# Where two head norms stand in VectorE's order: in front of a weight split or behind the running sums

## The reference, cut to what matters

```python
def _stick_breaking(q, k, v):
    for blk in range(seq // SB_BLOCK):
        ...
        z = jnp.einsum("bthd,bshd->bhts", qb, kb).astype(jnp.float32) * scale
        log_1m = jnp.where(causal, jax.nn.log_sigmoid(-z), 0.0)
        log_survive = lax.cumsum(log_1m, axis=3, reverse=True) - log_1m
        w = jnp.where(causal, jnp.exp(jax.nn.log_sigmoid(z) + log_survive), 0.0)
        outs.append(jnp.einsum("bhts,bshd->bthd", w.astype(vb.dtype), vb))

def _sb_mix(h, mem_n, w_in, q_g, k_g, w_out, mem_w_kv, mq_g, mk_g):
    q, k, v, q_mem = jnp.split(h @ w_in, [SB_WIDTH, 2 * SB_WIDTH, 3 * SB_WIDTH], axis=-1)
    q = _rmsnorm(q.reshape(shp), q_g)      # 12 heads of 128
    k = _rmsnorm(k.reshape(shp), k_g)
    o = _stick_breaking(q, k, v.reshape(shp)).reshape(b, s, SB_WIDTH)
    o_mem = _memory_attention(q_mem, mem_n, mem_w_kv, mq_g, mk_g)
    return jnp.concatenate([o, o_mem], axis=-1) @ w_out
```

## Time and profile before

| | |
|---|---|
| median of three runs | 805.43 us (805.22 to 806.25) |
| profiled execution, whole | 805.58 us |
| its span | 803.8 us |
| TensorE (PE) busy | 793.8 us, 99% of the span |
| VectorE (DVE) busy | 609.1 us, 76% |
| ScalarE (ACT) busy | 437.4 us, 54% |
| GpSimd (POOL) busy | 62.9 us, 8% |
| granted TensorE clock | 0.999 of full speed over the span |

### The profile page before, as it was taken

One profiled execution on the slowest core, in us unless ns is written; L12 is line 12 of the kernel. 1 busy time (PEld: TensorE's weight loads), 2 busy tenths in 40 slices (PEclk: granted clock), 3 DMA queues, 4 the chain that ended last, 5 costly groups with the idle time before them and its releaser, 6 DMA issues.

```text
span 803.8 us, 9752 instructions
## 1 busy us (share of the span) xinstructions
PE 793.8 (99%) x3778; PEld 663.4 (83%) x3778; DVE 609.1 (76%) x906; ACT 437.4 (54%) x520; POOL 62.9 (8%) x80
## 2 busy tenths in 40 slices
PE   9989999999999999999999999999999999999998
PEld 7977888888888888888888888888888888888886
DVE  6678989998757688889447968588666778888742
ACT  6657776366636445444426576757743644445430
POOL 4000003540000000000000000113220000000000
PEclk9999999999999999999999999999999999999999
DMA  7845366544445666665565644443435565665551
GB/s 245 287 145 173 107 215 217 176 135 147 157 158 179 190 207 190 187 200 198 176 202 166 201 157 157 157 131 132 150 130 169 180 206 178 192 209 188 180 208 52
DMA packets 85293, 141.38 MB, mean 176 GB/s; under 512 B 3406, under 2 KB 50672, under 8 KB 85248
## 3 DMA queue, kind: packets, MB, share of 16 engines
q1 hardware_dynamic: 84256, 139.60, 53.3%
q10 hardware_dynamic: 608, 1.06, 0.4%
q0 software_dynamic: 384, 0.11, 0.1%
HBM read 139.68 MB, written 1.07 MB: 175 GB/s over the span
## 4 chain that ended last, share of the span: by engine, by line
PE 79%; DVE 12%; ACT 3%; issue 3%; DMA 2%; SPq 0%; DVEq 0%; ACTq 0%
PE acc L1294 24%; PE acc L1296 24%; PE acc L1295 24%; DVE lo L952 4%; PE bank L1291 3%; DVE zs L1065 2%; DMA raw<-in_ssd_w_in 2%; ACT hi L632 1%; DVE seg L1085 1%; DVE seg L1093 1%; PE bank L1488 1%; PE bank L1466 1%; DVE hg L1085 1%; ACT sq L632 1%; ACT zs L632 1%
## 5 line engine op out<-in xcount | busy, mean ns | idle before, releaser
L952 DVE TENSOR_TENSOR lo<-raw,hi 128x2048 fp32r<-128x2048 f32 (+2 forms) x132 | 296.5, 2252 | 91.3 <-ACT hi L632 90.0
L632 ACT ACTIVATE hi<-raw 128x2048 fp32r<-128x2048 f32 (+2 forms) x132 | 244.7, 1861 | 95.9 <-DMA raw<-in_ffn_w_gate_up 44.3
L1294 PE MATMUL acc<-lo,aT_hi 128*128 128x512 f32 (+1 forms) x672 | 262.5, 391 | 1.5 <-DVE lo L952 1.2
L1296 PE MATMUL acc<-hi,aT_lo 128*128 128x512 f32 (+1 forms) x672 | 258.9, 385 | 0.0
L1295 PE MATMUL acc<-hi,aT_hi 128*128 128x512 f32 (+1 forms) x672 | 258.5, 385 | 0.0
L1294 PEld LDWEIGHTS acc<-lo,aT_hi 128*128 128x128 f32 x672 | 126.3, 188 | 26.9 <-issue 1.4
L1296 PEld LDWEIGHTS acc<-hi,aT_lo 128*128 128x128 f32 x672 | 126.2, 188 | 25.3
L1295 PEld LDWEIGHTS acc<-hi,aT_hi 128*128 128x128 f32 x672 | 126.4, 188 | 24.2
L1172 DVE STREAM_TRANSPOSE uT<-un 32x256 f32<-32x256 f32 x160 | 69.7, 436 | 2.6
L1294 PE MATMUL acc<-lo,uT_hi 128*128 128x512 f32 x176 | 68.8, 391 | 0.0
L1295 PE MATMUL acc<-hi,uT_hi 128*128 128x512 f32 x176 | 68.6, 390 | 0.0
(11 more groups left out here) (203 smaller groups left out, 845.3 us busy)
## 6 DMA issues: line engine op xcount, KB each, us to landing
raw<-in_ffn_w_gate_up SPq DMA_DIRECT2D x88, 512.0 KB, 4.8
raw<-in_ffn_w_down SPq DMA_DIRECT2D x22, 1024.0 KB, 4.9
raw<-in_sb_w_in SPq DMA_DIRECT2D x20, 1024.0 KB, 5.1
raw<-in_ssd_w_in SPq DMA_DIRECT2D x14, 1024.0 KB, 5.3
raw<-in_mem_w_kv SPq DMA_DIRECT2D x8, 1024.0 KB, 5.0
raw<-in_ssd_w_out SPq DMA_DIRECT2D x8, 1024.0 KB, 4.9
raw<-in_sb_w_out SPq DMA_DIRECT2D x8, 1024.0 KB, 4.9
seg<-cs_rows SPq DMA_DIRECT2D x6, 384.0 KB, 4.9
```

The source lines that it names most:

```text
L632: return nc.scalar.activation(out_, in_, func, **k)
L952: v.tensor_tensor(lo[w % RING][:, c], raw[w % RING][:, c], hi[w % RING][:, c].bitcast(F), ALU.subtract).then_inc(lo_ready, 1)
L1294: mm(ps, stat_hi, mov_lo, start=first, stop=False)
L1296: return mm(ps, stat_lo, mov_hi, start=False, stop=last)
```

## The change

The norms of q1 and q2 get a kind of their own, "hl", which is not in `EARLY` and so comes in list order, last in its unit. The other eight norms stay "hn". The function that is called is the same.

```diff
+LATE_NORMS = ["q1", "q2"]
 HEAD_NORMS = ["qm0", "km0", "km1", "qm1", "k0", "k1", "k2", "q0", "q1", "q2"]
...
     for n in HEAD_NORMS:
-        at(block_end("dtq1" if n == "qm0" else n) + 1, ("hn", n))
+        at(block_end("dtq1" if n == "qm0" else n) + 1, ("hl" if n in LATE_NORMS else "hn", n))
...
-NO_BANK = ("gate", "silu", "seg", "segm", "pn", "dt", "memsq", "memnorm", "sps", "zd", "hn", "tq", "ts")
+NO_BANK = ("gate", "silu", "seg", "segm", "pn", "dt", "memsq", "memnorm", "sps", "zd", "hn", "hl", "tq", "ts")
...
-                elif kind == "hn":
+                elif kind in ("hn", "hl"):
                     head_norm(step[1])
```

## The result

The changed kernel takes 812.62 us (median of 6 runs, 812.50 to 815.24), the kernel before 805.60 us in the same comparison (805.22 to 806.57). The ratio is 1.0093, 95% interval 1.0082 to 1.0103: **7 us slower**, where no measurable difference was forecast (805.5, range 804.4 to 806.7). The profiled execution has 812.50 us and a span of 810.7 us.

The account below looks back on a forecast made before the run. TensorE was taken to bound the kernel, with one removable wait at `O`: -0.81 us won, +0.86 for both groups of transposes held by longer norms, +0.05 in sum, giving 805.5 us, range 804.4 to 806.7.

Parts of the forecast that it names:

- What bounds the kernel: TensorE, busy 99%; its one wait at 500 to 625 us, 0.6 us before `O`, traced through masks to q1's norm.
- Gain of up to 0.81 us: Unit 83's subtractions and masks come earlier, `O` starts unhindered at 530.92, q1's transposes at 532.22 instead of 533.03.
- Norms later: Norms of q1 and q2 start behind the subtractions; their transposes, ready at 531.63 and 564.00, have 0.59 us to spare.
- what is late next: Behind the norms: L1200, L1201, split, `spb` masks, `sp_hi`, `sp_lo`; until 571.7 in unit 88, hidden by 0.5 us.
- What eats the 0.59 us: GpSimd's masks fall into both late norms; two small VectorE instructions pass in 1.42 us, making the norm 1.02 us longer.
- d: What the masks add to a late norm: 1.02 us forecast, 0 to 1.42 as bounds; transposes max(0, d - 0.59) late.
- Rival 3: Both masks run back to back, VectorE gets nothing through, 1.42 us added per norm: +0.85, 806.3 us; chance 0.16.
- rival 4: Small norm instructions keep GpSimd's masks out until the norm ends; `O` 1.35 and 2.1 us later, 808.9 us; chance 0.04.

Follow-up runs that it names:

- the last run: Against the kernel before: in unit 83 the two subtractions of C, and `zd` of unit 84, go ahead of the split of unit 85; 804.77 us against 805.55, ratio 0.9991.

## Why the prediction was wrong, point by point

**What bounds the kernel: right but for one link.** One wait of TensorE, worth 0.8 us at most, caused by the norm ahead of the subtractions: the trace of the last run is shorter by 0.78. But `O` in unit 84 had a second condition beside the masks, and the trace of before has a sign of it, in a view that the prediction does not use. The waits of the weight loads (PEld) of the kernel before, 500 to 625 us, have one row, and the timeline has that load:

```profile
PEld bank L1488 <- DVE spb L1201: 1.0, 1, 1.0
```

```profile
531.62 0.30 PEld L1488 LDWEIGHTS bank<-lsb,vn 128*128 128x128 f32 x2 [0.97 <-DVE spb L1201]
```

The row names VectorE's `spb`. That is no operand of `O`, and by the code only the bank ties the two. It is not what the load waited for in the end: the first L1201 was done at 530.78, the masks at 531.55, 0.07 before the load. So the prediction's reading of that one wait, the masks, holds; what it missed is the tie, which was met 0.14 us before `O` was due at 530.92 and so had next to no room for a later `zd`.

**Gain of up to 0.81 us: right in size, not reached here.** The masks end in time, but the wait that took the place of the old one is longer.

**"Norms later": the failing step.** It asked who waits for the norm, found the transposes with 0.59 us to spare, and left the queue behind the norm to "what is late next". There L1200 and L1201 are named, but followed only through what they write, `spb`, the masks, `sp_hi` and `sp_lo` to the next sums. They also free what they read. For unit 88 the prediction even has `zd` end at 567.0, and compares that only with the sums at 572.18. A late `zd` was put at nothing for `O`; it made `O` 2.7 us late in each place. With the bank as a condition the prediction's own numbers give the result: norm to 532.50, then 1.1 for the first two instructions of `zd`, 533.6 against an `O` due at 530.92, so 2.7 us late; in unit 88 566.0 against 563.28, again 2.7. Measured are 2.65 (533.36 against 530.48 + 0.23) and 2.66, of which 2.50 show as idle time. The transposes, which the forecast had waiting 0.43 us each, wait for nothing at all: `O` holds TensorE until long after the norm is done.

**What eats the 0.59 us: right.** d was put at 1.02, with two small instructions passing beside two masks. The trace has two at 0.66 and 0.67 instead of 0.17, 0.99 us together, and without the masks the wait shrinks by 1.0. The prediction cited the Trainium skill, "SBUF — State Buffer", section "Who interferes with whom", for a lock that excludes the other engine for a whole instruction; the 0.66 and 0.67 agree, and so does the 1.87 of the masks beside a split. L1141, whose 0.55 us the prediction counts as agreeing, reads only one tensor, so it is no instance of two inputs. Rival 3, in which VectorE gets nothing through between the two masks, did not happen.

**Chances.** Slower by over 0.2% had 0.04, for rival 4 or a large d. The slower case that came true was not among the rivals, because they were built on those who wait for the norm's output or for the masks. The range rested on the same two.

**What was left out besides: the clock.** A wait of 2.5 us can cost more than itself, here 4.0 instead of 2.4 us. That no wait of that length was foreseen is why it did not come up.

## What to carry to other kernels

When a step moves ahead of others on an engine, follow each of the steps behind it twice: who needs what it writes, and who needs the buffer that it reads. With a few PSUM banks given out in turn, the second list is found in the table of bank uses, four steps on, and it may name an instruction that shares no data with the step. A row in the waits of the weight loads that names an output which the matmul does not read is the sign of such a tie, even where another condition was met later. And a step that fills an engine's idle time is not free to move: taken out of it, the steps behind both come later by the time that is idle again. Here `zd`, behind the norm in both orders, came 2.75 us later, 1.59 of it idle time.

## What the runs showed of the hardware

The granted clock did not answer the same way to the same wait. Behind a wait of 2.50 us it averaged 0.67 over 535 to 540 us in the place of q1 and stayed 1.00 in the place of q2 in the profile of the changed kernel; with q1 alone late it stayed 1.00 in that place, with q2 alone late it averaged 0.68 in the other one. Of the two waits of 3.4 us with the norm behind `zd`, the first was followed by 0.50 for 5 us, which is 1.2 GHz, the second by 1.00; two waits of 1.51 us by 1.00 both. In the changed kernel the drop shows as 4.0 instead of 2.4 us for one wait. The runs with q1 alone, 807.66 and 807.96 against 808.97 to 809.31, lie apart by about as much. Their mean granted clocks are 1.000 and 0.999 against 0.998 for the three longer ones, so the drop came in some executions of one and the same kernel and not in others.

The Trainium skill, "TensorE: Matmul & The Clock Gate", section "Part 1: The HAM clock gate (the "warmup" mystery)", says that the activity is watched in a window that runs on its own and not from the kernel's start, so that the moment of a change depends on where the work falls in it. The two outcomes of one and the same wait agree with that; no run here moved the wait by itself to test it.

GpSimd and VectorE met as the rows of before had it: an instruction on 128 x 8 elements was held for the better part of a mask of 0.72 us, and where GpSimd's mask came second it waited out a split, 2.71 us for one mask in unit 84 of the changed kernel. With the sums first, the masks begin during the norm's reduction, which takes 1.22 us as without them (1.21), and the small instruction behind it, with one tensor input, takes 0.72 instead of 0.17. Moving either engine's order moves these meetings too, so that the length of a norm (5.1 to 6.1 us) is not a constant of the code.
